# Who does the first norm's work, and where three modulation chunks stand

## The chip, the cores and the metric

The kernel runs on one core of one Trainium2 chip. The metric is the device time of one execution in microseconds, and the numbers given are medians over executions. The core has five engines that run side by side, each with its own instruction stream: TensorE (PE: matmuls, weight loads shown as PEld), VectorE (DVE), ScalarE (ACT), GpSimd (POOL) and SyncE (SP), which here only issues DMAs. They wait for each other through semaphores.

## What is computed

Two transformer-like blocks over 256 tokens of width 1024, plus a 256-token memory and a 256-token context, all in float32. What matters here, cut from the reference:

```python
h = h + _hybrid_mixer(_rmsnorm(h, mix_norm_w[l]), positions, w_in[l], ...)      # first block
h = h + _memory_cross_attn(_rmsnorm(h, xattn_norm_w[l]), mem_n, wq, wk, wv, wo)
h = h + _conv_ffn(_rmsnorm(h, ffn_norm_w[l]), ffn_up[l], ffn_conv_w[l], ffn_down[l])

def _rmsnorm(x, w):
    return (x * lax.rsqrt(jnp.mean(x * x, axis=-1, keepdims=True) + EPS)) * w

def _memory_cross_attn(h, mem_n, wq, wk, wv, wo):                                # 4 heads of 256
    q, k, v = h @ wq, mem_n @ wk, mem_n @ wv
    return softmax(q @ k.T * 256 ** -0.5) @ v @ wo

def adaln(cvec, w_mod, b_mod):                   # second block: 9 * 1024 columns for each of 2 layers
    return jax.nn.silu(cvec) @ w_mod + b_mod
```

The hybrid mixer's first branch (retention) rotates its queries and keys by angles from `positions`.

## The kernel before, in words

Activations lie feature-major: 8 tiles (`k`) of 128 features by 256 tokens. Weights come from HBM as chunks of 128x2048 floats (1 MB) through one ring of three raw slots; SP issues one DMA for each chunk, in a fixed list (`loads`, built from `plan` and `MODS_BEHIND`). To reach float32 accuracy each weight chunk `raw` is split in two: ScalarE writes the rounded `w_hi` (`split_hi`, L234), VectorE the remainder `w_lo` (`split_lo`, L242). Activations are split in the same way into `xn_hi` and `xn_lo`, and every product is three matmuls (L258 to L260): 48 for a chunk of two output tiles at 256 tokens. A raw slot is free for the next DMA once `lo_ready` has counted its chunk (L219 ff.), so VectorE's place in its own stream decides when SP may issue a load.

Each engine's stream is an order written out by hand. No planner is behind it. The prologue:

- SP: residual `xc`, eight small tables (`START`), chunks 0, 1, 2, the memory `xc[C]`, chunk 3 (waits for `lo_ready` 1), chunk 4 (waits for `lo_ready` 2), and right behind chunk 4 the nine mixer tables (`load_mixer_tables`, L529; the last is `gt<-in_pos`, the positions).
- ScalarE: eight squares (L344), `w_hi` of chunks 0 and 1, root table load and first guess (L388, L390), its square (L392), `xn_hi` for 8 tiles (L401), `w_hi` of chunk 2, squares of the memory.
- GpSimd: adds of the first norm's squares (L369; with `direct=5` two adds, and the rest is summed by TensorE), later five adds for the memory norm.
- TensorE: sum over partitions with a matrix of -1 (L373 for the added tile, L376 once for each tile that was not added), then chunk 0 tile by tile as `xn_lo` arrives, chunk 1, the memory norm's sum, chunk 2, the retention's turned products (L584, L585), and `v_tok` transposes (L591), which wait for ScalarE's copy of chunk 2 (L1403).
- VectorE: `w_lo` of chunks 0 and 1, one Newton step (L413, L415), then a scale (L431) and a low part (L438) for each k, `w_lo` of chunk 2, then the retention angles (L539 to L545), whose first step waits for all nine mixer tables.

The modulation matrix `w_mod` is read as 72 chunks (`mod`, L1644: eight small matmuls each), in six groups of 12, put between other stages by `MODS_BEHIND`: `{name: {c: (count, ahead)}}` means that `count` of them run behind chunk `c` of that job, and that their loads stand `ahead` chunks later in the list. Three stand behind the first attention (`wq` chunk 3), three within `a1_up0` (behind its chunks 2 and 5). `Attention.pe` runs eight units (4 heads, 2 token tiles each) in this order for unit u: scores of u+2, transposes of u, for even u values of head u/2-1. It has a hook `after_unit(u)`.

Of the kernel before, what the change touches and what calls it, by code (L numbers as in the profile page):

```python
# [41 lines left out]
ACT = mybir.ActivationFunctionType  # L42
# [6 lines left out]
KT = D // P  # L49
# [21 lines left out]
MODS_BEHIND = {  # L71
    "w_in_g": {3: (12, 2)},
    "wk": {3: (1, 1)},
    "wq": {3: (3, 2)},
    "wo": {3: (2, 2)},
    "ffn_down1": {7: (3, 2)},
    "a1_up0": {2: (2, 1), 5: (1, 1)},
    "a1_up1": {c: (2, 1) for c in (3, 7)},
    "a1_down1": {0: (2, 1), 3: (2, 1), 5: (1, 1), 7: (3, 2)},
    "ab_u": {1: (3, 2)},  # L80
# [9 lines left out]
def mods_behind(name, c):  # L90

    return MODS_BEHIND.get(name, {}).get(c, (0, 1))[0]
# [36 lines left out]
def build(nc, io, plan):  # L129
# [23 lines left out]
    with ExitStack() as ctx:  # L153
# [31 lines left out]
        X = slice(0, T)  # L185
# [5 lines left out]
        def col(name, k=0):  # L191
            return small[:, cols[name] + k:cols[name] + k + 1]
# [12 lines left out]
        def landed(load):  # L205

            at = place[load]
            return raw_landed[at % SLOTS], 16 * (at // SLOTS) + 16

        def raw_slot(load):  # L210
            return place[load] % SLOTS
# [14 lines left out]
        def split_hi(act, g):  # L226

            if g >= total:
                return
            slot, size = g % SLOTS, sizes[g]  # L230
            act.wait_ge(*landed(("main", g)))
            if g >= SLOTS:
                act.wait_ge(chunk_done, g + 1 - SLOTS)
            act.activation(w_hi[:, slot, 0:size], raw[:, raw_slot(("main", g)), 0:size], ACT.Copy).then_inc(hi_ready, 1)  # L234

        def split_lo(dve, g):

            if g >= total:
                return
            slot, size = g % SLOTS, sizes[g]  # L240
            dve.wait_ge(hi_ready, g + 1)
            dve.tensor_tensor(w_lo[:, slot, 0:size], raw[:, raw_slot(("main", g)), 0:size], w_hi[:, slot, 0:size].bitcast(F32),  # L242
                              ALU.subtract).then_inc(lo_ready, 1)

        def first_splits(eng, split):

            for g in range(2):
                split(eng, g)

        def bank_free(pe, s):  # L250

# [68 lines left out]
        class Norm:  # L320

            made, scaled, split, squared, added = 0, 0, 0, 0, 0
# [289 lines left out]


        _, XT, NT, QT, _, BR, GR, RT = (area(i * 1024, 8) for i in range(8))


# [91 lines left out]
        def delta_pool(pool):  # L708
            need(pool, "gdn_dve", "unit")
            pool.memset(XT, 0.0).then_inc(inverse_zero, 1)  # L710
# [202 lines left out]
        def delta_pe_u0(pe, o):  # L913
            pe.wait_ge(level_x, 15)
            pe.wait_ge(inverse_full, 4)
            for h, _, f in heads4:
                mm = pe.matmul(psum[:, 3, f], XT[:, h, :], v_tok[:, 0, f], start=True, stop=True)
            o(mm, "u0")
# [13 lines left out]
        def delta_pe_u1(pe, o):  # L932
            need(pe, "gdn_dve", "rest")
            for h, _, f in heads4:
                mm = pe.matmul(psum[:, 1, f], XT[:, 4 + h, :], REST[:, f], start=True, stop=True)
            o(mm, "u1")
# [177 lines left out]
        def gated_pool_first(pool):  # L1114
            pool.wait_ge(n_lo, memory.split_base + KT)
            pool.memset(resets, 1.0).then_inc(resets_set, 1)
            pool.wait_ge(resets_set, 1)
            pool.memset(resets.rearrange("p (b l) -> p b l", l=RUN)[:, :, 0], 0.0).then_inc(resets_set, 1)
# [512 lines left out]
        def mods_pe(pe, n):  # L1631


            for m in range(mods_run[0], mods_run[0] + n):
                group, j = m // MOD_GROUP, m % MOD_GROUP
                if j == 0:
                    if m == 0:
                        pe.wait_ge(mod_act, 1)
                    else:
                        pe.wait_ge(mod_taken, group)  # L1640
                pe.wait_ge(*landed(("mod", m)))
                for k in range(KT):
                    q = slice(32 * (k % 4), 32 * (k % 4) + 32)
                    mm = pe.matmul(psum[q, 7, 0:256], c_pad[:, k, C_AT - 2 * j:C_AT - 2 * j + 32],  # L1644
                                   raw[:, raw_slot(("mod", m)), k * 256:(k + 1) * 256],
                                   start=(j == 0 and k < 4), stop=(j == MOD_GROUP - 1 and k >= 4), tile_position=(0, 32 * (k % 4)),
                                   skip_group_check=True)
                    if k >= 4:
                        mm.then_inc(mod_used, 1)
            mods_run[0] += n  # L1650
# [534 lines left out]
        k_all = qk12[:, 8:12, :].rearrange("p (h w) t -> p h (w t)", w=2)  # L2185


        first = Norm(X, lambda k, h: col("mix_norm_w", k), direct=5)
        memory = Norm(C, lambda k, h: col("mem_norm_w", k), tiles=2, pool_low=True)
        cross = Norm(X, lambda k, h: col("xattn_norm_w", k), tiles=2)  # L2190
        ffn = Norm(X, lambda k, h: col("ffn_norm_w", k), tiles=2, early_table=True, first_tile=0)
# [12 lines left out]
        att1 = Attention(4, 2, T, lambda h, i: q1[:, 2 * h + i, :], lambda h, i: k1[:, 2 * h + i, :], lambda h, j: v1[:, j, h * T:(h + 1) * T])  # L2204
# [7 lines left out]
        @block.sync  # L2212
        def _(sp):
            sp.dma_start(xc[:, :, X], io["x"]).then_inc(residual_in, 16)
            for name in START:
                sp.dma_start(START[name][:], io[name]).then_inc(start_in, 16)
            for at in range(len(loads)):
                load(sp, at)
                if at == SLOTS - 1:
                    sp.dma_start(xc[:, :, C], io["mem"]).then_inc(mem_in, 16)  # L2220
                if loads[at] == ("main", 4):
                    load_mixer_tables(sp)

            sp.wait_ge(out_ready, 1)
            sp.dma_start(io["out"][:, 0:KT // 2, :], nrm[:, 0:KT // 2, X]).then_inc(out_in, 16)
            sp.wait_ge(out_in, 32)

        @block.tensor
        def _(pe):
# [92 lines left out]
            cross.ready(pe, KT - 1)  # L2322
            pe_feature_major(pe, jobs["wq"], xn_hi, xn_lo, X)
            pe.wait_ge(evacuated, jobs["wq"].base + jobs["wq"].n)
            att1.pe(pe)
            mods_pe(pe, mods_behind("wq", 3))
            pe.wait_ge(at_lo, att1.heads)
            pe_feature_major(pe, jobs["wo"], xn_hi, xn_lo, X, in_halves={3: pe_tile_by_tile})
            ffn.pe(pe)
# [61 lines left out]
        def _(act):  # L2391
            act.wait_ge(residual_in, 16)
            first.act_squares(act)
            act.wait_ge(start_in, 16 * len(START))
            first_splits(act, split_hi)
            first.act_rest(act)
            act.wait_ge(mem_in, 16)
            split_hi(act, 2)
            act.wait_ge(n_lo, first.split_base + KT)
# [130 lines left out]
        def _(dve):  # L2530
            dve.memset(zeros[:, :], 0.0).then_inc(set_up, 1)
            dve.memset(c_pad[:, :, :], 0.0).then_inc(set_up, 1)
            dve.wait_ge(set_up, 2)
            first_splits(dve, split_lo)
            dve.wait_ge(start_in, 16 * len(START))
            first.dve(dve)
            ret_order, delta_order, gated_order = order(dve, "ret_dve"), order(dve, "gdn_dve"), order(dve, "gat_dve")
            split_lo(dve, 2)
            retention_dve_angles(dve, ret_order)
# [172 lines left out]

        @block.gpsimd
        def _(pool):
            first.pool(pool)
            memory.pool(pool)
            memory.pool_lows(pool)
            gated_pool_first(pool)
            delta_pool(pool)
            cross.pool(pool)  # L2720
            ffn.pool(pool)
            feed0.pool(pool, lambda: n20c.pool(pool))
            n20.pool(pool)
            feed1.pool(pool)
            n21.pool(pool)
            n22.pool(pool)
            feed2.pool(pool)
            n23.pool(pool)
            feed3.pool(pool)
            n24.pool(pool)  # L2730
            n25.pool(pool)
            feed4.pool(pool)
            last.pool(pool)
# [223 lines left out]
```

## Time and profile before

| | |
|---|---|
| median of 3 runs | 2179.31 us (2178.08 to 2181.6) |
| profiled execution | 2182.45 us, its span 2180.6 us |
| PE busy | 2108.1 us, 97% of the span |
| DVE, ACT, POOL busy | 984.9, 817.2, 224.7 us |
| chain that ended last | PE 87%, DVE 7%, ACT 3%, issue 2% |
| mean granted TensorE clock | 0.991 |
| DMA | 313.97 MB, mean 144 GB/s |

The span is what the profile covers; the 1.8 us between it and the execution's own time lie around it. Busy times are sums over the whole span and say nothing on one stage. TensorE is busy nearly always, so what counts is the few places where it is not, or where its granted clock is 0.50 instead of 1.00.

### The profile page before, as it was taken

How to read it: one execution, taken by the hardware profiler on the slowest of the kernel's cores; microseconds unless marked ns; L12 is line 12 of the kernel's file. 1: busy time of each engine (PE TensorE's matmuls, PEld its weight loads, DVE VectorE, ACT ScalarE, POOL GpSimd, SP SyncE). 2: the span in 40 equal slices, each digit the busy share in tenths (PEclk: the TensorE clock that was granted, in tenths of full speed). 3: DMA queues.
4: the chain of work that ended last, by engine and by line, in shares of the span. 5: the costliest groups of instructions: out<-in, count | busy, mean ns of one | idle time of the engine just before them, and what ended most of it. 6: DMA issues, size and time to landing. Idle time of an engine off the chain costs nothing.

```text
span 2180.6 us, 31782 instructions
## 1 busy us (share of the span) xinstructions
PE 2108.1 (97%) x13882; PEld 1818.8 (83%) x13882; DVE 984.9 (45%) x1270; ACT 817.2 (37%) x1044; POOL 224.7 (10%) x185
## 2 busy tenths in 40 slices
PE   7988999999999999999999999999999999999998
PEld 6985998999978888788887888888778888869998
DVE  6677555767522322354542332243232235645444
ACT  5642454555522222243332222233212224445344
POOL 1000001413101001100101001111000110001001
PEclk9999999999999999999999999999999999999999
DMA  6425544554641243452343332243334222364543
GB/s 235 154 79 195 202 183 174 170 186 155 225 149 67 104 154 114 157 196 97 126 164 129 114 115 81 87 161 135 136 125 154 75 81 100 117 251 155 166 178 112
DMA packets 53707, 313.97 MB, mean 144 GB/s; under 512 B 5952, under 2 KB 12352, under 8 KB 23744
## 3 DMA queue, kind: packets, MB, share of 16 engines
q1 hardware_dynamic: 50848, 308.98, 39.8%
q10 hardware_dynamic: 2720, 2.95, 0.4%
q8 instruction: 109, 1.79, 0.3%
q14 instruction: 30, 0.25, 0.0%
HBM read 310.86 MB, written 1.05 MB: 143 GB/s over the span
## 4 chain that ended last, share of the span: by engine, by line
PE 87%; DVE 7%; ACT 3%; issue 2%; DMA 0%; SPq 0%; POOL 0%; DVEq 0%; ACTq 0%; POOLq 0%
PE psum L258 26%; PE psum L259 26%; PE psum L260 26%; PE psum L1644 3%; DVE w_lo L242 2%; ACT w_hi L234 2%; PE psum L1293 1%; PE psum L1283 1%; DVE work L431 0%; PE psum L1307 0%; DMA raw<-in_w_in_r 0%; DVE work L719 0%; DVE xn_lo L1809 0%; PE psum L895 0%; PE psum L1712 0%
## 5 line engine op out<-in xcount | busy, mean ns | idle before, releaser
L258 PE MATMUL psum<-xn_hi,w_hi 128*128 128x256 f32 (+1 forms) x2600 | 863.9, 332 | 22.1 <-DVE xn_lo L438 7.8
L259 PE MATMUL psum<-xn_lo,w_hi 128*128 128x256 f32 (+1 forms) x2600 | 853.1, 328 | 0.0
L260 PE MATMUL psum<-xn_hi,w_lo 128*128 128x256 f32 (+1 forms) x2600 | 852.7, 328 | 0.0
L242 DVE TENSOR_TENSOR w_lo<-raw,w_hi 128x2048 fp32r<-128x2048 f32 (+1 forms) x246 | 510.0, 2074 | 456.5 <-ACT w_hi L234 455.6
L258 PEld LDWEIGHTS psum<-xn_hi,w_hi 128*128 128x128 f32 x2600 | 496.4, 191 | 78.5 <-issue 25.5
L259 PEld LDWEIGHTS psum<-xn_lo,w_hi 128*128 128x128 f32 x2600 | 496.8, 191 | 42.6 <-issue 1.0
L260 PEld LDWEIGHTS psum<-xn_hi,w_lo 128*128 128x128 f32 x2600 | 496.5, 191 | 42.3
L234 ACT ACTIVATE w_hi<-raw 128x2048 fp32r<-128x2048 f32 (+1 forms) x246 | 421.7, 1714 | 219.6 <-PE psum L260 136.6
L258 PE MATMUL psum<-h_hi,w_hi 128*128 128x512 f32 (+1 forms) x913 | 314.9, 345 | 1.8 <-POOL h_lo L1619 1.7
L259 PE MATMUL psum<-h_lo,w_hi 128*128 128x512 f32 (+1 forms) x913 | 313.2, 343 | 0.0
L260 PE MATMUL psum<-h_hi,w_lo 128*128 128x512 f32 (+1 forms) x913 | 313.1, 343 | 0.0
L1619 POOL TENSOR_TENSOR h_lo<-work,h_hi 128x512 fp32r<-128x512 f32 (+1 forms) x110 | 154.6, 1406 | 1146.8 <-ACT h_hi L1551 1146.8
L1540 ACT ACTIVATE work<-psum 128x512 f32<-128x512 f32 (+1 forms) x88 | 47.9, 544 | 476.9 <-PE psum L260 476.8
L1589 DVE TENSOR_TENSOR work<-work,psum 128x512 f32<-128x512 f32 (+1 forms) x88 | 54.7, 621 | 373.2 <-ACT work L1540 373.1
L258 PEld LDWEIGHTS psum<-h_hi,w_hi 128*128 128x128 f32 x913 | 171.7, 188 | 27.0 <-issue 2.5
L259 PEld LDWEIGHTS psum<-h_lo,w_hi 128*128 128x128 f32 x913 | 171.8, 188 | 22.5
L260 PEld LDWEIGHTS psum<-h_hi,w_lo 128*128 128x128 f32 x913 | 171.7, 188 | 22.4
L1474 DVE SCALAR_TENSOR_TENSOR xc<-psum,mods,xc 128x256 f32<-128x256 f32 x126 | 55.7, 480 | 184.8 <-PE psum L260 184.5
L369 POOL TENSOR_TENSOR work<-work 128x256 f32<-128x256 f32 (+1 forms) x60 | 62.2, 1037 | 722.6 <-ACT work L360 673.1
L360 ACT ACTIVATE work<-xc 128x512 f32<-128x512 f32 (+2 forms) x42 | 26.1, 622 | 187.6 <-DVE xc L1474 166.3
L1551 ACT ACTIVATE h_hi<-work 128x512 fp32r<-128x512 f32 (+1 forms) x110 | 60.1, 547 | 81.4 <-DVE work L1589 81.4
L1644 PE MATMUL psum<-raw,c_pad 128*32 128x256 f32 x1152 | 73.6, 383 | 0.0
(374 smaller groups left out, 1334.0 us busy)
## 6 DMA issues: line engine op xcount, KB each, us to landing
raw<-in_mod SPq DMA_DIRECT2D x72, 1024.0 KB, 4.8
raw<-in_a_up SPq DMA_DIRECT2D x42, 1024.0 KB, 4.9
raw<-in_b_up SPq DMA_DIRECT2D x42, 1024.0 KB, 4.8
raw<-in_ffn_up SPq DMA_DIRECT2D x22, 1024.0 KB, 4.8
raw<-in_a_down SPq DMA_DIRECT2D x32, 704.0 KB, 4.1
raw<-in_b_down SPq DMA_DIRECT2D x32, 704.0 KB, 4.1
raw<-in_ffn_down SPq DMA_DIRECT2D x16, 704.0 KB, 4.2
raw<-in_wo SPq DMA_DIRECT2D x8, 1024.0 KB, 4.8
```

Of the source, the lines that this page charges most:

```text
L234: act.activation(w_hi[:, slot, 0:size], raw[:, raw_slot(("main", g)), 0:size], ACT.Copy).then_inc(hi_ready, 1)
L242: dve.tensor_tensor(w_lo[:, slot, 0:size], raw[:, raw_slot(("main", g)), 0:size], w_hi[:, slot, 0:size].bitcast(F32), ALU.subtract).then_i ...
L258: pe.matmul(out, lh, rh, start=first, stop=False, skip_group_check=group)
L259: pe.matmul(out, lh, rl, start=False, stop=False, skip_group_check=group)
L260: return pe.matmul(out, ll, rh, start=False, stop=last, skip_group_check=group)
L369: pool.tensor_tensor(nrm[:, 0, 0:self.w], nrm[:, 0, 0:self.w], nrm[:, k, 0:self.w], ALU.add).then_inc(n_added, 1)
L1474: mm = dve.scalar_tensor_tensor(x, got, gate[:, tile, h], x, ALU.mult, ALU.add)
L1540: act.activation(b[r, 0, 0:self.w], psum[r, s.bank, 0:self.w], ACT.Silu).then_inc(ff_gate, 1)
L1551: act.activation(out, b[r, 1:2, 0:self.w], ACT.Copy).then_inc(ff_hi, 1)
L1589: dve.tensor_tensor(b[r, 1, 0:self.w], b[r, 0, 0:self.w], up[up_r], ALU.mult).then_inc(evacuated, 1)
L1619: pool.tensor_tensor(lo, b[r, 1:2, 0:self.w], hi.bitcast(F32), ALU.subtract).then_inc(ff_lo, 1)
L1644: mm = pe.matmul(psum[q, 7, 0:256], c_pad[:, k, C_AT - 2 * j:C_AT - 2 * j + 32], raw[:, raw_slot(("mod", m)), k * 256:(k + 1) * 256], star ...
```

## The change

In the prologue VectorE adds the first norm's squares, six adds where GpSimd had two, so that TensorE sums two tiles in place of six. ScalarE loads its root table and makes the guess and its square ahead of both weight splits, which now stand between the high parts. VectorE does the Newton step and three scales ahead of its first weight split, and the second weight split stands behind the fifth low part. Separately, three modulation chunks move from `a1_up0` to the first attention: one behind each of units 4, 5 and 6, and three behind the attention as before.

```diff
@@ MODS_BEHIND
-    "wq": {3: (3, 2)},
+    "wq": {3: (6, 2)},
-    "a1_up0": {2: (2, 1), 5: (1, 1)},
@@ the norms
-        first = Norm(X, lambda k, h: col("mix_norm_w", k), direct=5)
+        first = Norm(X, lambda k, h: col("mix_norm_w", k), direct=1, early_table=True)
@@ tensor
-            att1.pe(pe)
-            mods_pe(pe, mods_behind("wq", 3))
+            att1.pe(pe, lambda u: mods_pe(pe, 1) if 4 <= u < 7 else None)
+            mods_pe(pe, mods_behind("wq", 3) - 3)
@@ scalar
-            first_splits(act, split_hi)
-            first.act_rest(act)
+            act.activation(col("tables", first.j), col("freq"), ACT.Abs_reciprocal_sqrt)
+            first.act_guess(act)
+            split_hi(act, 0)
+            first.act_high(act, range(0, 2))
+            split_hi(act, 1)
+            first.act_high(act, range(2, KT))
@@ vector
-            first_splits(dve, split_lo)
+            first.pool(dve)
             dve.wait_ge(start_in, 16 * len(START))
-            first.dve(dve)
+            first.dve_stats(dve)
+            for k in range(3):
+                first.dve_scale(dve, k)
+            split_lo(dve, 0)
+            for k in range(KT):
+                first.dve_low(dve, k)
+                if k + 3 < KT:
+                    first.dve_scale(dve, k + 3)
+                if k == 4:
+                    split_lo(dve, 1)
@@ gpsimd
-            first.pool(pool)
```

Line numbers after the change are six lower around the norms (L431 becomes L425, L438 becomes L432), one lower at the splits (L242 becomes L241).

VectorE's stream at the start, before (the third row holds `w_lo` of chunks 0 and 1):

```order
L2531 MEMSET zeros 128x256
L2532 MEMSET c_pad 128x432
L242 TENSOR_TENSOR w_lo<-raw,w_hi 128x2048 x2
L413 SCALAR_TENSOR_TENSOR half<-psum,half 128x256
L415 SCALAR_TENSOR_TENSOR rstd<-half,rstd 128x256
L431 SCALAR_TENSOR_TENSOR work<-xc,small,rstd 128x256 x2
L438 TENSOR_TENSOR xn_lo<-work,xn_hi 128x256
```

The same place after the change, up to the first low part, and further on from the last scale to the first step of the angles (`gt` holds the positions):

```order
L363 TENSOR_TENSOR work<-work 128x256 x6
L407 SCALAR_TENSOR_TENSOR half<-psum,half 128x256
L409 SCALAR_TENSOR_TENSOR rstd<-half,rstd 128x256
L425 SCALAR_TENSOR_TENSOR work<-xc,small,rstd 128x256 x3
L241 TENSOR_TENSOR w_lo<-raw,w_hi 128x2048
L432 TENSOR_TENSOR xn_lo<-work,xn_hi 128x256
...
L425 SCALAR_TENSOR_TENSOR work<-xc,small,rstd 128x256
L241 TENSOR_TENSOR w_lo<-raw,w_hi 128x2048
L432 TENSOR_TENSOR xn_lo<-work,xn_hi 128x256 x3
L241 TENSOR_TENSOR w_lo<-raw,w_hi 128x2048
L533 CAST work<-gt 128x256
```

The `w_lo` of chunk 1, which stood ahead of the whole norm, now stands behind the last scale; the order of everything from `w_lo` of chunk 2 on is as it was. SP's stream, after the change as before it, is the following between chunk 3 and chunk 5 (`w_in_d` x2 are chunks 3 and 4):

```order
L223 DMA raw<-in_w_in_d 128x2048 x2
L523 DMA minus_head<-in_minus_head 128x128
L523 DMA head_rows<-in_head_rows 128x168
L523 DMA in_run<-in_in_run 128x128
L523 DMA triu<-in_triu 128x128
L523 DMA tril_strict<-in_tril_strict 128x128
L523 DMA second_half<-in_second_half 128x384
L523 DMA decay<-in_decay 128x1024
L523 DMA gk_up<-in_gk_up 128x128
L523 DMA gt<-in_pos 128x256
L223 DMA raw<-in_w_in_d 128x2048
```

Nothing moved in it; the nine tables stand behind the load of chunk 4.

TensorE in the first attention from unit 4 on, before (L1283 scores, L1307 transposes, L1293 values, L1644 modulation) and after (the same four are L1277, L1301, L1287, L1638):

```order
L1307 MATMUL psum<-ident,work 128x128 x2
L1293 MATMUL psum<-work,z 128x256 x4
L1283 MATMUL psum<-z 128x256 x2
L1307 MATMUL psum<-ident,work 128x128 x4
L1293 MATMUL psum<-work,z 128x256 x4
L1307 MATMUL psum<-ident,work 128x128 x2
L1293 MATMUL psum<-work,z 128x256 x4
L1644 MATMUL psum<-raw,c_pad 32x256 x24
```

```order
L1301 MATMUL psum<-ident,work 128x128 x2
L1287 MATMUL psum<-work,z 128x256 x4
L1638 MATMUL psum<-raw,c_pad 32x256 x8
L1277 MATMUL psum<-z 128x256 x2
L1301 MATMUL psum<-ident,work 128x128 x2
L1638 MATMUL psum<-raw,c_pad 32x256 x8
L1301 MATMUL psum<-ident,work 128x128 x2
L1287 MATMUL psum<-work,z 128x256 x4
L1638 MATMUL psum<-raw,c_pad 32x256 x8
L1301 MATMUL psum<-ident,work 128x128 x2
L1287 MATMUL psum<-work,z 128x256 x4
L1638 MATMUL psum<-raw,c_pad 32x256 x24
```

The first of the three added chunks stands ahead of the scores of unit 7, the second ahead of the transposes of unit 6, the third ahead of those of unit 7.

## Rows read from the trace of the kernel before

**Rows 1.** Waits of TensorE, 20 to 135 us: total, times, longest (us)

```profile
PE psum L258 <- DVE xn_lo L438: 6.2, 1, 6.2
PE psum L837 <- DVE work L727: 2.9, 1, 2.9
...
PE psum L591 <- ACT z L1403: 0.9, 1, 0.9
```

**Rows 2.** Chain that ended last, 20 to 60 us: start, duration (us), what

```profile
29.05 0.76 DVE work L539
...
33.96 0.42 ACT work L579
...
43.11 0.59 ACT z L1403
43.74 0.66 PE psum L591 x4
...
53.03 1.62 PE psum L599 x16
```

**Rows 3.** Timeline of the prologue: start, duration (us), engine, line, what, idle before

```profile
6.38 2.56 ACT L344 ACTIVATE work<-xc 128x256 f32<-128x256 f32 x8 [4.36 <-DMA xc<-in_x]
...
9.92 4.47 PE L376 MATMUL psum<-work,minus 128*128 128x256 f32 x10
...
13.33 4.64 DVE L242 TENSOR_TENSOR w_lo<-raw,w_hi 128x2048 fp32r<-128x2048 f32 x2 [11.74 <-ACT w_hi L234]
...
17.06 0.46 ACT L390 ACTIVATE rstd<-psum,small 128x256 f32<-128x256 f32 x1
...
19.99 0.43 DVE L438 TENSOR_TENSOR xn_lo<-work,xn_hi 128x256 fp32r<-128x256 f32 x1
...
20.57 0.55 PE L258 MATMUL psum<-xn_hi,w_hi 128*128 128x256 f32 x1 [6.17 <-DVE xn_lo L438]
```

**Rows 4.** Timeline of SP's queue, 0 to 60 us

```profile
15.65 2.67 SPq L224 DMA_DIRECT2D raw<-in_w_in_d  x2
...
22.44 0.44 SPq L529 DMA_DIRECT2D gt<-in_pos  x1
```

**Rows 5.** DMA issues: count, KB each, us to landing (chunk 5; positions; a late table)

```profile
raw<-in_w_in_d SPq DMA_DIRECT2D x1, 1024.0 KB, 5.0
...
gt<-in_pos SPq DMA_DIRECT2D x1, 128.0 KB, 5.1
...
ax_cos<-in_ax_cos ACTq DMA_DIRECT2D x1, 128.0 KB, 2.0
```

**Rows 6.** Timeline of GpSimd and VectorE, 26 to 38 us

```profile
27.32 5.86 POOL L369 TENSOR_TENSOR work<-work 128x256 f32<-128x256 f32 x5 [18.53 <-ACT work L344]
...
26.76 2.29 DVE L242 TENSOR_TENSOR w_lo<-raw,w_hi 128x2048 fp32r<-128x2048 f32 x1 [1.38 <-ACT w_hi L234]
...
31.60 0.85 DVE L543 TENSOR_SCALAR work<-work 128x256 f32<-128x256 f32 x1
...
36.62 0.29 DVE L551 TENSOR_SCALAR work<-work 128x256 f32<-128x256 f32 x1
```

**Rows 7.** Stretches: us, busy (x) of PE, PEld, DVE, ACT, POOL, PEclk, DMA, GB/s

```profile
20.50:24.50 4.00, 3.93 (x18) 3.96 (x19) 4.00 (x12) 2.09 (x5) 0.00 (x0) 0.50 1.00 378
24.50:28.70 4.20, 4.20 (x37) 4.20 (x36) 2.68 (x3) 4.20 (x6) 1.38 (x1) 0.98 0.50 190
...
82.80:84.00 1.20, 1.20 (x8) 1.20 (x7) 1.20 (x1) 1.19 (x2) 0.00 (x0) 0.50 0.66 280
```

**Rows 8.** Timeline of the first attention, units 6 and 7, and the modulation behind it

```profile
330.24 0.41 DVE L1354 TENSOR_REDUCE small<-psum 128x1 f32<-128x256 f32 x1
...
331.35 0.44 PE L1307 MATMUL psum<-ident,work 128*128 128x128 f32 x2 [1.31 <-DVE work L1369]
...
336.41 2.80 PE L1644 MATMUL psum<-raw,c_pad 128*32 128x256 f32 x48
```

**Rows 9.** Timeline of TensorE in `a1_up0`, one modulation chunk behind chunk 5

```profile
641.92 1.07 PE L1644 MATMUL psum<-raw,c_pad 128*32 128x256 f32 x16
```

More of the change, by code:

```diff
@@ L243, in split_lo @@
                               ALU.subtract).then_inc(lo_ready, 1)
-        def first_splits(eng, split):
-            for g in range(2):
-                split(eng, g)
         def bank_free(pe, s):
```

## The prediction, made before the changed kernel was run

> **What bounds the kernel now.** TensorE is busy 97% of the span, so I looked first for where it stands still near the two edits, in its waits: 6.2 us ahead of the first weight matmul, 0.9 us ahead of the transposes L591, 2.9 us at L837 [rows 1]. The first of these is what the prologue edit seems to be worth. Whether it is, the chain of waits tells. Followed back from L591 at 43.74 it does not go to the early matmuls. It goes to ScalarE's copy of chunk 2 at 43.11, which stands behind the memory norm, and that behind the sines at 33.96, which wait for VectorE's angles, begun at 29.05 [rows 2]. From 43.74 TensorE works without a pause until the scores L599 at 53.03, and the chain goes through them and on to the DVE-bound wait at L837. So the prologue's end is worth what it moves L591, and that hangs on the six angle steps: when they begin and how fast they run. TensorE's own matmuls of chunks 0 to 2 have 0.9 us to spare before L591 and no more weight than that.
>
> **Prologue: when TensorE starts.** The second square is done at 7.1 (eight in 2.56 us from 6.38). A two-input 128x256 step takes VectorE 0.43, about 0.46 with its semaphore; six make 2.8, so the adds end at 9.9. TensorE did ten half-passes of such a sum in 4.47; now four are left, so the sum is there at about 12.0, and the guess, at 17.06 before, stands at 12.05 [rows 3]. The first scale follows 2.0 later as it did, three of them end at 15.3, and `w_lo` of chunk 0 takes 2.3 (two in 4.64): 17.5. Its `w_hi`, begun behind the guess's square at 12.95, is ready by 14.9. The first matmul comes 0.58 behind the start of the first low part as before: 18.05 against 20.57. So TensorE starts 2.5 us earlier. VectorE's steps of this part follow each other at 0.36 (11 starts in 4.00 us) [rows 7], so the fifth low part and the last scale are done at 21.1, and `w_lo` of chunk 1 at 23.35. TensorE is at its lower clock at first (18 matmuls in 4.00 us against 37 in 4.20) [rows 7] and waits some 0.5 us for the sixth low part. Chunks 0 to 2 and the turned products end about 2.1 us earlier, at 40.8 against 42.9.
>
> **Prologue: what is late next.** The load of chunk 4 waits for `w_lo` of chunk 1. That was done at 18.0, in the middle of the two issues that begin at 15.65 and take 2.67; it is 23.4 now, 5.4 us later, and the nine tables are queued behind that load. The positions, issued at 22.44 (4.45 behind chunk 4), are issued at 27.8 [rows 4]. They landed 5.1 after issue; a table on an empty queue took 2.0. That bounds the landing by 29.8 and 32.9 [rows 5]. I take 31.5: a 1 MB load on an empty queue took 5.0 [rows 5], so chunk 4 is there at 28.4, and the nine tables, 1.27 MB by their shapes, take 3.1 more at about 400 GB/s (378 in the stretch of rows 7, where the queue was full). VectorE, done with `w_lo` of chunk 2 at 26.7, stands idle until then. The angles begin 2.5 us later than at 29.0.
>
> **Prologue: what is faster.** GpSimd's five adds of the memory norm lay beside the angles, 27.32 to 33.2. In that time a one-input step took 0.85, and the same form 0.29 once they were over [rows 6]. After the change the memory's squares begin 24.5 in place of 26.6, so the adds run from 25.2 and are over by 31.1 even at the old pace, before the angles begin. The six steps took 4.9 (29.05 to 33.96, rows 2). Alone they take 0.33 each for three one-input steps, 0.46 each for two two-input ones, and 0.45 for the cast, which I bound by the two rows, 0.29 and 0.85: 2.35. The angles then end at 33.85, where they ended at 33.9. The late tables and the gone neighbour cancel: L591 moves by -0.1 us.
>
> The Trainium skill (GPSIMD Engine Reference, the specification table) says that GpSimd's way to SBUF is shared with VectorE, with contention for VectorE's two-port modes and for steps with two SBUF inputs. The trace agrees for the one-input steps, which it would call a two-port mode, and not for the other half: the two-input `w_lo` beside the adds took its usual 2.29 [rows 6]. By that rule alone `w_lo` of chunk 2, which now lies beside the adds too, might be slowed; it hides before the late tables, so the sum stays.
>
> **Prologue: the clock.** TensorE now has about 2.85 us without work ahead of L591 (40.8 to 43.65), before 0.9. The one wait of such a length in the same stretch, 2.9 us at L837 [rows 1], was followed by a granted clock of 0.50, that is 1.2 GHz [rows 7]. At that level a stretch of work takes twice as long; 3 to 4 us of it cost 1.5 to 2. I take 1.5. It lies on the path, since TensorE has no pause between L591 and L599. Bounds: 0 (no fall) and 2.0 (the 4 us stretch of rows 7). Prologue in sum: -0.1 + 1.5 = +1.4; from -1.8 (tables at 29.8, no fall) to about +3.5 (tables at 32.9, 2.0 for the clock).
>
> **Modulation.** In `a1_up0` TensorE does nothing but matmuls back to back. A modulation chunk there took 1.0 [rows 9] and some 0.05 around it; three take 3.0 and are saved. Behind the attention three took 2.7 (336.41 to 339.1), 0.87 each [rows 8]. Inside, the first stands ahead of the scores of unit 7. Their row maximum is what VectorE did at 330.24 ahead of normalising unit 6, for which TensorE waited 1.31 at 331.35 [rows 8]. So the first delays that chain by its whole 0.87 and hides nothing; the second then lies in the 1.31 wait and is hidden; the third delays the values of the last head, less some 0.2 of the wait there. The attention grows by 1.5. The loads: the third added chunk frees its slot at about 335.2, so the last modulation chunk lands at 340.1, while TensorE could take it at 339.6; 0.4 is waited. 1.9 less 3.0 is -1.1 us. Bounds: -3.0 (all hidden) and 0 (none, and the load late).
>
> **Sum.** +1.4 - 1.1 = +0.3 us against the profiled execution: 2182.45 + 0.3 = 2182.75. That execution lies 3.1 above the median of the runs, so I forecast 2179.31 + 0.3, rounded down to 2179.5.
>
> **Rivals.**
>
> 1. The tables only cost their latency. With an almost empty queue `gt` lands 2.0 behind its issue, at 29.8; the angles end at 32.2, L591 is 1.7 earlier and the idle time before it 1.3 us, near the 0.9 of before [rows 1], so the clock should stay up. -1.8 - 1.1: 2176.4. For: all nine are small. Against: 5.0 for one load alone on the queue, and they are behind one. [...] Chance 15%.
> 2. Slower: the angle steps keep their 4.9 us, since what slowed them was the queue's or ScalarE's traffic and not GpSimd. Tables at 31.5, angles end at 36.4, L591 is 2.5 later; TensorE is idle 5.5 us and the clock costs 2.0. +4.5 - 1.1 = +3.4: 2182.7, and 2184.1 with the tables at 32.9. It decides at any pace above 0.6 for a one-input step without GpSimd. Against it stands the 0.29 row. Chance 15%.
> 3. The gain that the wait promises: 2.5 us of earlier start arrive at L591, because the tables do not matter. -2.5 - 1.1: 2175.7. Against: VectorE waits for all nine by its code, and SP cannot issue them before 23.4. Chance 5%.
> 4. The attention does not take the three chunks (late loads or a longer chain), and the modulation edit gives nothing: +1.4: 2180.7. Chance 10%.
>
> **How the numbers follow.** The forecast has 55%. A difference under 0.2%, 4.4 us, is what a measurement of this kernel can hardly tell from none; 2175.0 to 2183.7 is that band. The forecast and rivals 3 and 4 lie inside it, rival 1 too, rival 2 reaches over its upper edge. The later clock falls may shift with the phase, by 1.5 each. So: same 0.80, faster 0.10, slower 0.10. The range is 2175.7 to 2183.5: rival 3's time below, a late rival 2 above.
>
> **What would show it.** Right: the first weight matmul near 18; chunk 4 issued near 23.4 and the positions near 27.8; VectorE idle for 4 to 5 us ahead of the cast; one-input angle steps of 0.3; L591 near 43.6 behind a longer wait, and a clock of 0.50 right after; six modulation chunks behind and in the attention that end 1.9 later, against the attention's start; `a1_up0` 3.0 shorter. Wrong: the cast right behind `w_lo` of chunk 2; steps of 0.85; L591 off by over 1.5 us; a new wait in `a1_up0` or in `wo`.

## The result, and the profile after

The changed kernel takes 2183.26 us (median of 20 executions, 2180.27 to 2186.95) against 2179.49 (20, 2176.83 to 2182.95) for the kernel before on the same chip. The ratio is 1.0015, with a 95% interval of [1.0008, 1.0021] (every ratio below is given in this way). By the ratio that is some 3.3 us more, by the medians 3.8. A later comparison gave 2183.34 against 2179.8, 1.0013 [1.0004, 1.0021]. That is within 0.2%, just inside the upper end of the forecast range (2183.5), and real: the interval excludes 1.

The two profiled executions alone don't show it: that of the changed kernel took 2181.04 us, less than that of before (2182.45). So they are compared stage by stage. Lines of the changed kernel stand 6 lower than before around the norms (L585 is what L591 was, L593 the scores L599, L831 the old L837).

The timeline of the prologue after (start, duration in us, engine, line, operation, idle before), against [rows 3], [rows 4] and [rows 6]:

```profile
6.61 2.56 ACT L338 ACTIVATE work<-xc 128x256 f32<-128x256 f32 x8 [4.58 <-DMA xc<-in_x]
7.44 3.07 DVE L363 TENSOR_TENSOR work<-work 128x256 f32<-128x256 f32 x6 [5.85 <-ACT work L338]
...
12.74 0.47 ACT L384 ACTIVATE rstd<-psum,small 128x256 f32<-128x256 f32 x1 [2.06 <-PE psum L370]
...
15.91 2.29 DVE L241 TENSOR_TENSOR w_lo<-raw,w_hi 128x2048 fp32r<-128x2048 f32 x1
...
21.77 2.28 DVE L241 TENSOR_TENSOR w_lo<-raw,w_hi 128x2048 fp32r<-128x2048 f32 x1
```

```profile
18.23 6.18 SPq L223 DMA_DIRECT2D raw<-in_w_in_d  x2
```

```profile
25.80 5.59 POOL L363 TENSOR_TENSOR work<-work 128x256 f32<-128x256 f32 x5 [25.36 <-ACT work L338]
```

The guess is there 4.3 us earlier (12.74 for 17.06), and TensorE's first weight matmul starts at 18.68 for 20.57. But `w_lo` of chunk 1 ends at 24.05, and the second of SP's two loads, chunk 4, goes out then: its issue row runs from 18.23 to 24.41. The chain that ended last (start, duration, what), against [rows 2], shows what follows:

```profile
24.08 0.33 SPq L223
...
28.26 4.26 DMA gt<-in_pos
32.54 0.30 DVE work L533
...
34.37 0.43 DVE work L539
34.83 0.43 ACT work L573
...
43.98 0.59 ACT z L1397
44.61 1.12 PE psum L585 x4
...
56.51 1.62 PE psum L593 x16
```

The table queue begins at 24.45 behind chunk 4, the positions are issued at 28.26 and land 4.3 later, and only then does VectorE begin the angles. Its six steps take 2.3 us (32.54 to 34.83) where before they took 4.9. From the end of the angles to the transposes it is 9.78 us in both kernels (33.96 to 43.74, 34.83 to 44.61). So L585 is 0.9 late. From it to the scores it is another matter: 9.29 us before (43.74 to 53.03), 11.90 now. The stretches (busy and count of PE, PEld, DVE, ACT, POOL, then granted clock, DMA share, GB/s) say why, and the waits of TensorE (total, times, longest) say what came ahead:

```profile
PE psum L585 <- ACT z L1397: 3.2, 1, 3.2
PE psum L831 <- DVE work L721: 2.8, 1, 2.8
```

```profile
44.60:49.00 4.40, 4.39 (x21) 4.39 (x22) 2.61 (x2) 1.76 (x1) 0.98 (x2) 0.50 0.02 7
49.00:53.00 4.00, 4.00 (x30) 4.00 (x30) 3.90 (x4) 0.00 (x0) 0.00 (x0) 0.81 0.80 268
```

After 3.2 us without work TensorE runs at a granted clock of 0.50 (1.2 GHz) until about 50.5, 21 matmuls in 4.4 us.

The first attention after (timeline of TensorE), against [rows 8]:

```profile
318.55 2.86 PE L1277 MATMUL psum<-z 128*128 128x256 f32 x12 [0.75 <-ACT z L1433]
...
330.84 1.07 PE L1638 MATMUL psum<-raw,c_pad 128*32 128x256 f32 x16
...
333.12 1.07 PE L1638 MATMUL psum<-raw,c_pad 128*32 128x256 f32 x16
334.13 0.44 PE L1301 MATMUL psum<-ident,work 128*128 128x128 f32 x2
...
336.23 1.07 PE L1638 MATMUL psum<-raw,c_pad 128*32 128x256 f32 x16
...
338.15 1.99 PE L1287 MATMUL psum<-work,z 128*128 128x256 f32 x8 [0.47 <-ACT work L1315]
340.07 1.93 PE L1638 MATMUL psum<-raw,c_pad 128*32 128x256 f32 x32
343.07 1.07 PE L1638 MATMUL psum<-raw,c_pad 128*32 128x256 f32 x16 [1.07 <-DMA raw<-in_mod]
344.08 0.39 PE L252 MATMUL psum<-xn_hi,w_hi 128*128 128x256 f32 x1
```

From the first scores to the first `wo` matmul it takes 25.53 us. Before it took 22.52, by these two rows of the same view:

```profile
316.61 2.86 PE L1283 MATMUL psum<-z 128*128 128x256 f32 x12 [0.75 <-ACT z L1439]
...
339.13 0.39 PE L258 MATMUL psum<-xn_hi,w_hi 128*128 128x256 f32 x1
```

To see what each stage is worth I followed one kind of instruction, VectorE's weight splits (246 in each kernel, always in the same order), and took the difference of the n-th start in two traces. Three pairs, before and after, in us: split 8, 61.59 and 65.08 (+3.5); split 34, just ahead of the attention, 312.63 and 314.58 (+2.0); split 88, behind `a1_up0`, 701.02 and 702.75 (+1.7). The modulation edit is the last step, -0.2. Rows of the third pair (VectorE, before and after):

```profile
701.02 2.20 DVE L242 TENSOR_TENSOR w_lo<-raw,w_hi 128x1408 fp32r<-128x1408 f32 x1
```

```profile
702.75 2.20 DVE L241 TENSOR_TENSOR w_lo<-raw,w_hi 128x1408 fp32r<-128x1408 f32 x1
```

The drop from +3.5 to +2.0 lies at 83 us, where before has a stretch at 0.50 [rows 7] and after has none. Past 1800 us three more such stretches differ in place and length, and the difference ends at -1.4. Those are the ways in which one execution differs from the next, as the second pair of profiles shows below.

### The profile page after: what moved, and what is told of

It is laid out like the page before. It is cut to its first block, busy times and chain, and to the rows that moved or that the text cites. A ratio compares the mean times of both kernels' runs of the same rounds, so it can differ in the third digit from the quotient of the medians.

```text
span 2179.2 us, 31773 instructions
## 1 busy us (share of the span) xinstructions
PE 2102.7 (96%) x13874; PEld 1814.2 (83%) x13874; DVE 983.9 (45%) x1276; ACT 816.5 (37%) x1044; POOL 222.5 (10%) x183
## 4 chain that ended last, share of the span: by engine, by line
PE 85%; DVE 7%; ACT 4%; issue 2%; DMA 1%; SPq 0%; DVEq 0%; ACTq 0%
PE psum L252 26%; PE psum L254 25%; PE psum L253 25%; PE psum L1638 3%; DVE w_lo L241 2%; ACT w_hi L233 2%; PE psum L1287 1%; PE psum L1277 1%; DMA raw<-in_mod 0%; DVE work L425 0%; PE psum L1301 0%; DVE work L713 0%; DVE xn_lo L1803 0%; PE psum L889 0%; DVE work L994 0%
## 5 line engine op out<-in xcount | busy, mean ns | idle before, releaser
L241 DVE TENSOR_TENSOR w_lo<-raw,w_hi 128x2048 fp32r<-128x2048 f32 (+1 forms) x246 | 509.8, 2073 | 435.9 <-ACT w_hi L233 435.1
L1638 PE MATMUL psum<-raw,c_pad 128*32 128x256 f32 x1152 | 74.0, 383 | 1.4 <-DMA raw<-in_mod 1.4
```

## The experiments

### The prologue alone, the modulation alone

Prologue alone: the kernel before with the edits of the prologue. Modulation alone:

```diff
-    "wq": {3: (3, 2)},
+    "wq": {3: (6, 2)},
-    "a1_up0": {2: (2, 1), 5: (1, 1)},
-            att1.pe(pe)
-            mods_pe(pe, mods_behind("wq", 3))
+            att1.pe(pe, lambda u: mods_pe(pe, 1) if 4 <= u < 7 else None)
+            mods_pe(pe, mods_behind("wq", 3) - 3)
```

> The changed prologue alone; the modulation chunks stand as in the kernel before. Theory (late tables, then the clock): the tables land near 32.5 us, the transposes L591 start 0.9 us later than before (near 44.6), TensorE's clock falls in the wait ahead of them, and the time is 2 to 4 us above the kernel before, as for the whole change. Rival (the modulation move is what costs): this one is at or below the kernel before, by up to 2 us, and the other half carries the loss.

> The three modulation chunks moved into the attention alone; the prologue is as before. Theory: the attention, from its first scores to the first matmul of wo, grows by 3.0 us (1.0 for each chunk inside, 0.9 saved of a wait, 1.1 waited for the last chunk's load and the rest behind), a1_up0 loses 3.0, and the time is within 1 us of the kernel before. Rival (the move is what costs): 2 us or more above it. My forecast had 1.1 us below.

The prologue alone: 2182.92 us against 2180.94, 1.0011 [1.0002, 1.0020]. Its timeline:

```profile
33.56 0.29 DVE L534 CAST work<-gt 128x256 f32<-128x256 int32 x1 [6.39 <-DMA gt<-in_pos]
```

```profile
45.63 1.12 PE L586 MATMUL psum<-ident,z 128*128 128x128 f32 x4 [4.34 <-ACT z L1398]
```

Here the positions landed 5.4 behind their issue at 28.17, so the transposes came 1.9 late, not the expected 0.9. But the clock was at 0.50 for half as long, and the scores stood near the same place as in the whole change, +3.2 against before (split 8: +3.2).

The modulation alone: 2178.6 us against the same 2180.94, 0.9996 [0.9988, 1.0005]. The attention grew by 3.1, split 88 against split 34 is -0.3, and the same load was waited for:

```profile
340.42 1.07 PE L1643 MATMUL psum<-raw,c_pad 128*32 128x256 f32 x16 [1.15 <-DMA raw<-in_mod]
```

So the whole loss is the prologue's, and the modulation edit is worth nothing that can be measured.

### The tables behind chunk 3 instead of chunk 4

The whole change with one more line, and the prologue alone with the same line:

```diff
-                if loads[at] == ("main", 4):
+                if loads[at] == ("main", 3):
                     load_mixer_tables(sp)
```

> The whole change, with the nine mixer tables issued behind chunk 3 in place of chunk 4. Theory: the positions are issued near 23.1 us and are there before VectorE has done w_lo of chunk 2 (27.3); the angles run beside GpSimd's five adds at 0.85 for a one-input step and end near 32.2 in place of 34.8; L591 comes near 42.0, with under 1.5 us of idle time ahead of it and the clock still up; the time is 1 to 3 us below the kernel before and 4 to 6 below the changed one. Rival (the tables are not what L591 waits for): no more than 1 us below the changed kernel. Second rival (the angle steps are slow or fast by the DMA traffic beside them): they take 0.3 here too and end near 29.6.

> The changed prologue with the tables behind chunk 3, and the modulation chunks as before. Theory: the same as with the whole change and early tables within 1 us, since the modulation move gives nothing: 1 to 3 us below the kernel before. If the modulation move costs, this one is the best of all by 1 us or more; if it gains its 1.1, it is 1 us above the one with the whole change.

The whole change with the line takes 2178.88 us, 0.9991 [0.9982, 0.9999], and the prologue alone with it 2178.16, 0.9989 [0.9981, 0.9998], both against 2180.94. One line turns the loss into a small gain; so it was the tables' place in the queue. The two are alike, so here too the modulation edit gives nothing. The timeline of the first:

```profile
24.96 2.29 DVE L241 TENSOR_TENSOR w_lo<-raw,w_hi 128x2048 fp32r<-128x2048 f32 x1
27.16 0.29 DVE L533 CAST work<-gt 128x256 f32<-128x256 int32 x1
27.49 0.71 DVE L534 TENSOR_SCALAR work<-work,small 128x256 f32<-128x256 f32 x1
28.24 0.85 DVE L536 TENSOR_SCALAR work<-work 128x256 f32<-128x256 f32 x1
...
30.00 0.97 DVE L538 SCALAR_TENSOR_TENSOR work<-work 128x256 f32<-128x256 f32 x1
```

```profile
41.67 0.66 PE L585 MATMUL psum<-ident,z 128*128 128x128 f32 x4 [0.30 <-ACT z L1397]
```

```profile
41.70:45.00 3.30, 3.30 (x28) 3.30 (x29) 1.54 (x1) 1.72 (x1) 0.95 (x2) 1.00 0.02 7
```

The angles start behind `w_lo` of chunk 2 without waiting, beside GpSimd's adds (25.79 to 31.57), and all but the cast are slow again: 4.7 us for the six. Even so L585 comes 2.1 earlier than before, TensorE waits 0.3, and its clock stays up.

### How long the angle steps take without GpSimd's adds

The kernel before, with one addition on GpSimd for the memory norm instead of five (TensorE sums the rest):

```diff
-        memory = Norm(C, lambda k, h: col("mem_norm_w", k), tiles=2, pool_low=True)
+        memory = Norm(C, lambda k, h: col("mem_norm_w", k), tiles=2, direct=6, pool_low=True)
```

> The kernel before, with GpSimd adding one tile for the memory norm in place of five; TensorE sums seven in place of three. Theory (GpSimd's adds are what doubled the angle steps): L540, L542 and L543 take near 0.3 us in place of 0.85, the six steps 2.3 to 3 in place of 4.9, though the tables are as early as before. Rival (the DMA traffic or ScalarE beside them): they stay at 0.85.

One profile, 2180.29 us. VectorE's and GpSimd's rows:

```profile
28.79 0.83 DVE L539 CAST work<-gt 128x256 f32<-128x256 int32 x1
29.66 0.35 DVE L540 TENSOR_SCALAR work<-work,small 128x256 f32<-128x256 f32 x1
30.05 0.29 DVE L542 TENSOR_SCALAR work<-work 128x256 f32<-128x256 f32 x1
...
30.71 0.42 DVE L544 SCALAR_TENSOR_TENSOR work<-work 128x256 f32<-128x256 f32 x1
```

```profile
27.14 2.33 POOL L369 TENSOR_TENSOR work<-work 128x256 f32<-128x256 f32 x1 [18.30 <-ACT work L344]
```

The cast, which overlaps the end of the one addition (29.47), is slow; everything behind it is at the fast pace, and the six steps take 2.8 us. On VectorE nothing was changed, so GpSimd's adds are what slows them. Two-input steps too: 0.42 here, 0.97 beside the adds. In return GpSimd's addition took 2.33 while `w_lo` ran beside it. An addition without `w_lo` beside it takes 0.74; this is the third of the five in the kernel before:

```profile
30.68 0.74 POOL L369 TENSOR_TENSOR work<-work 128x256 f32<-128x256 f32 x1
```

There the two engines take turns: the slow one-input steps end at 30.69, 31.57 and 32.45, and the next additions begin at 30.68, 31.56 and 32.45. So a small step beside the adds takes about as long as one add.

This kernel shows only the pace of the steps. Its transposes L591 came 1.1 us later than before, with no wait ahead of them, since TensorE had the longer sum (2.75 us for 1.03) and was itself the last to be ready.

### The wait before L585 filled with work

The whole change, and three needless matmuls (into a free bank) between the turned products and the transposes:

```diff
             retention_pe_turned(pe, ret_order)
+            for _ in range(3):
+                pe.matmul(bank(5), rot[:, :], decay[:, 0:2, :], start=True, stop=True)
             retention_pe_values(pe, ret_order)
```

> The whole change, with three needless matmuls (128x512, into an unused bank) between the turned products and the v_tok transposes, in the time in which TensorE otherwise waits; their results are used by nothing. Theory (the tables cost 0.9 us, the clock the larger part): the matmuls take 0.9 each and end before the copy of chunk 2, the transposes start near 44.6 us as in the changed kernel, but the clock is still up, so the scores L593 come 9.3 us behind them (53.9) in place of 11.9 (56.5); the time is 1.5 to 3 us below the changed kernel. Rival (the clock is not what costs; the loss is the later start alone): no more than 0.5 us below the changed kernel, and the scores near 56.5.

It took 2182.42 us against 2181.93, 1.0005 [0.9996, 1.0014].

```profile
41.50 2.74 PE L2235 MATMUL psum<-decay,rot 128*128 128x512 f32 x6
44.90 0.66 PE L585 MATMUL psum<-ident,z 128*128 128x128 f32 x4 [0.66 <-ACT z L1397]
```

```profile
45.00:49.00 4.00, 4.00 (x35) 4.00 (x36) 2.32 (x2) 1.64 (x1) 0.87 (x2) 1.00 0.00 0
```

The transposes came no earlier (44.90 against 44.61), but the clock stayed at 1.00, the scores stood 9.27 behind them instead of 11.90, and split 8 is at +1.1 instead of +3.5. Idle time ahead of L585 costs more than itself: here the clock's part was 2.6, the larger of the two terms. The median moved the right way, but its interval holds both 1 and the changed kernel's ratio; the term's size rests on the traces.

### Two chunks inside the attention, with the early tables

```diff
-    "wq": {3: (3, 2)},
+    "wq": {3: (5, 2)},
-    "a1_up0": {2: (2, 1), 5: (1, 1)},
+    "a1_up0": {2: (1, 1)},
-            att1.pe(pe)
-            mods_pe(pe, mods_behind("wq", 3))
+            att1.pe(pe, lambda u: mods_pe(pe, 1) if u in (3, 5) else None)
+            mods_pe(pe, mods_behind("wq", 3) - 2)
```

> Changed prologue, tables behind chunk 3, and another place for the modulation: one chunk behind each of units 3 and 5 of the attention, three behind it, one left in a1_up0. Theory (a chunk is hidden only where TensorE waits for VectorE, and a late load costs): the one of unit 5 is hidden in the 1.3 us wait, the one of unit 3 is not, the loads are in time; the attention to wo grows by 1.1 us where a1_up0 loses 2.0, and the time is 0.5 to 1.5 below the kernel with early tables and the modulation as before, which the times can hardly show. Rival (any chunk inside costs its full 1.0 us): no gain.

> The same kernel as e6 once more. Its first time was 6 to 8 us below the kernel before, where its moved work explains 4.7 (as the chunks' weight splits stood at 1790 us). Theory (the rest was where the clock's falls lay late in the program, which differs between executions): the median falls back toward 4 to 6 us below the kernel before, and the profile again shows 4.7 +- 0.5 at 1790 us once the prologue's clock stretches are taken off. Rival (the other place of the modulation also takes clock falls away for good): again 6.5 us or more below.

It took 2173.59 us against 2181.93, 0.9970 [0.9958, 0.9983], and in the second comparison, of the same kernel, 2175.88 against 2179.8, 0.9982 [0.9973, 0.9990]. TensorE's timeline in the second:

```profile
324.28 1.07 PE L1639 MATMUL psum<-raw,c_pad 128*32 128x256 f32 x16
...
329.37 1.07 PE L1639 MATMUL psum<-raw,c_pad 128*32 128x256 f32 x16
330.75 0.44 PE L1302 MATMUL psum<-ident,work 128*128 128x128 f32 x2 [0.31 <-DVE work L1364]
...
335.80 2.80 PE L1639 MATMUL psum<-raw,c_pad 128*32 128x256 f32 x48
```

The chunk behind unit 5 stands where TensorE waited 1.31 us; the three behind the attention run in one piece, with no load waited for. The attention, from its first scores to `wo`, grew by only 0.5 us (22.52 to 23.06) where 1.1 was expected: the chunk behind unit 3 was partly hidden too, since the 0.45 us that TensorE waited ahead of unit 4's transposes in the kernel before (at 326.79) are gone. From split 34 to split 88 the two profiles give -1.6 each, and split 8 is at -1.9 and -2.2. Together that is 3.5 to 3.8 us; the second interval, 2.2 to 5.9 us of gain, holds it, and the first, 3.7 to 9.2, touches it. The expectation for the second run was missed: at 1790 us its weight splits are 2.8 ahead of the kernel before and not 4.7, and the median is 3.9 below it and not 4 to 6. This version beats both kernels. That it beats the two with early tables is shown by the traces' -1.6 alone, since the intervals of the times overlap with theirs. Which of its three differences from the whole change (two chunks, the other units, one load fewer) makes the modulation's gain was not tried apart.

### Both kernels profiled once more

> The kernel before once more, to see what differs between two executions of one program. Theory: the prologue and the waits fall at the same times within 0.5 us, but the stretches at the lower clock differ in place and number, and with them the span by 1 to 3 us. Rival: the same stretches as in the first profile.

> The changed kernel once more. Theory: tables near 32.5 us, L585 near 44.6 to 45.6, a stretch at the lower clock of 3.4 to 6.8 us that begins within the wait; 3 to 4 us above the kernel before in the median. Rival (the fall of the clock there was chance): the clock stays up in this profile, and the scores follow the transposes after 9.3 us.

The kernel before took 2183.99 us in its one execution. Its input landed 0.3 later and its first weight chunk 0.8, and its first stage ended later with them (split 8: +0.75 against the first profile, where at most 0.5 was expected; L591 at 44.50). The changed kernel took 2183.34 us in 12 executions (the ratio is above). Its timeline and the stretch:

```profile
33.47 0.29 DVE L533 CAST work<-gt 128x256 f32<-128x256 int32 x1 [6.31 <-DMA gt<-in_pos]
```

```profile
45.54 1.11 PE L585 MATMUL psum<-ident,z 128*128 128x128 f32 x4 [4.27 <-ACT z L1397]
```

```profile
44.60:49.00 4.40, 3.46 (x16) 3.46 (x17) 1.68 (x1) 2.69 (x3) 1.90 (x3) 0.61 0.20 84
49.00:53.00 4.00, 4.00 (x36) 4.00 (x35) 3.93 (x4) 0.00 (x0) 0.00 (x0) 1.00 0.58 184
```

The same two terms again, divided otherwise: the transposes are 1.8 late, the clock is back at 49, split 8 is at +3.3. Here the wait of 2.84 us at L831 was followed by 0.50, as before and unlike the first profile of the changed kernel: right behind it the difference is still +3.3 (split 13), where the first profile had +2.0. So the drop there was that execution's luck and no part of the change. In the twelve profiles of all kernels this wait was followed by the lower clock nine times; without it were the first of the changed kernel, one with early tables and one with two chunks inside.

## Why the prediction was right, and which terms were off

The forecast was no change within 0.2%, +0.3 us; it is +0.15% [+0.08, +0.21], about +3.3. In the prologue the mechanism was the one predicted, but it cost more than forecast; the modulation's gain did not come. By the traces the terms add up to about what was measured:

| term | predicted | first profile | second | prologue alone |
|---|---|---|---|---|
| transposes L591 move | -0.1 | +0.9 | +1.8 | +1.9 |
| clock behind them | +1.5 | +2.6 | +1.5 | +1.4 |
| modulation | -1.1 | -0.2 | -0.1 | |
| sum | +0.3 | +3.3 | +3.2 | +3.2 |

(The moves are against 43.74, the first profile of the kernel before; the clock's term is the time from the transposes to the scores less the 9.29 of before. The three profiles with the old prologue and all its adds have the transposes at 43.4, 43.7 and 44.5, so the first row is uncertain by some 0.8. The sum is clear of that: split 8 differs from the first profile by -0.3 to +0.8 in those three and by +3.2 to +3.5 with the new prologue.)

- **TensorE's earlier start.** Right that it is worth nothing. It was 1.9 us instead of 2.5: the input landed 0.2 later, six adds took 3.07 and not 2.8. With the first add 0.1 later behind its square, some 0.65 came through to `w_lo` of chunk 1, done at 24.05 for 23.4.
- **What is late next.** The mechanism was right: chunk 4 waits, and nine tables behind it. The size was off. I took the positions at 31.5; they came at 32.5, 33.5 and 33.5 in the three profiles of this prologue with unfilled wait (32.8 with it filled). Of the 1.0 to 2.0, 0.3 to 0.5 is the later issue. The rest is the landing, 4.3 to 5.4 us behind the issue, where I had allowed 3.7 by summing sizes at the queue's rate. The row of before, 5.1 [rows 5], was the better estimate, and I had chosen under it. The 2.0 of the late table was no row for this case: it went out on ScalarE's queue (ACTq), alone.
- **What is faster.** Right: six steps in 2.29 for 2.35. The rival that gave the slowing to something else fell with the one-addition kernel. That rule of the Trainium skill on the shared way to SBUF (GPSIMD Engine Reference, the specification table) named steps with two SBUF inputs too. My "not for the other half", from `w_lo` alone, was a misreading: the two-input L538 and L539 take 0.97 and 0.84 beside the adds and 0.42 without, and where `w_lo` keeps its 2.29 it is the add beside it that waits, 2.33 for 0.74.
- **The clock.** Right in kind, with a bound too low: I capped it at 2.0 by the 4 us stretch of [rows 7]. In the first profile the work behind the wait ran at the lower level from 44.6 to about 50.5. In the three profiles the two terms trade: where the tables are later, this term is smaller, and the sum to the scores is +3.2 to +3.5 each time, near the +3.5 that the prediction had as the prologue's upper bound. Why the clock comes back after another length of time was not settled.
- **Modulation.** This step failed: -1.1 was forecast, and -0.1 to -0.3 is what the traces show. The two chunks ahead of unit 6's transposes cost 0.84 (14.74 us from the first scores to them before, 15.58 now): as predicted, the 1.31 wait hides one. The third cost 0.89 and not 0.67 (from unit 6's transposes to the last values it is 4.02 us, and 3.13 before, 331.35 to 334.48): a chunk alone between other work takes 1.0, as [rows 9] had it, and I had used the 0.87 of a row of three. The last load cost 1.1 and not 0.4: its slot comes free with that third chunk at 337.2, and it lands 5.8 later, at 343.0, where I had allowed 4.9. The attention grew by 3.0 for 1.9, and `a1_up0` gave 3.2 back for 3.0. So rival 4, an edit without gain, is what held for this part.
- **Rivals.** Tables at their mere latency (29.8) and a gain of 2.5 from the early start did not occur. Rival 2's price, +3.4, was met by other means than its own: the steps ran at 0.29 to 0.35 without the adds.

Of the chances, the 0.80 for within 0.2% held. The forecast's value lies 3.8 below the measured median, since the terms together came out on the costly side of what I took: the transposes and the modulation each time, the clock in the first profile. That the median is inside the range at all is in part luck: it lies 0.2 below the upper end, which was set for rival 2, the slow steps, and that did not occur. (That end is also below the rival's own 2184.1, and the terms named for the prologue's upper bound, 1.3 and 2.0, sum to 3.3 and not 3.5.)

## What to carry to other kernels

When a step is moved ahead of another on one engine, look for the semaphore counts of the one that is pushed back: here a weight split freed a load slot, and what stood behind that load in SP's queue, not the load, was the loss; one line put it right. Do not take a landing time below what the same transfer took in the trace unless the queue ahead of it gets shorter. The waits of 3.2 to 4.3 us ahead of these transposes carried a surcharge of 1.4 to 2.6 us at the lower clock, so a small lateness there is to be priced at more than itself. And fill the waits of an engine with as many pieces as they hold, not one more. Before reading a small difference from two single profiles, profile each kernel twice: here the same stage of the same kernel moved by 0.8 us, and whole spans of one kernel differed by 1.6 to 4.4.

## What was not expected of the hardware

- The same wait in the same code is not always followed by the lower clock: 2.84 us at L831 was, in the second profile of the changed kernel (0.50 from 87.0 to 89.4), and was not in the first (1.00 from 86.0 on). It was in nine profiles of twelve.
- The lower clock lasted longer after the shorter wait: after 3.2 us until about 50.5 us, after 4.3 us until 49.
- At the start of the changed kernel TensorE works at the pace of the lower level, 20 matmuls in 4.3 us, in a stretch whose granted clock reads 1.00. So the mean granted clocks of the two kernels (0.991 and 0.994) are not to be compared.

```profile
18.70:23.00 4.30, 4.30 (x20) 4.30 (x21) 4.30 (x10) 2.79 (x6) 0.00 (x0) 1.00 0.67 244
```

- The contention of VectorE and GpSimd works both ways: a 128x256 addition on GpSimd took 2.33 us beside a 128x2048 `w_lo`, which itself kept its 2.29, while VectorE's small steps took two to three times as long beside the same adds. The cast is the exception: right behind `w_lo` it took 0.29 in three profiles with early tables, though the first add had not ended, and 0.83 in others.
- The same 128 KB table, issued at 28.1 to 28.3 behind the same transfers, landed 4.3 us later in one execution and 5.3 and 5.4 in two others. The table issued just ahead of it landed at 31.7 to 31.8 in all three, so it is the last one alone that varied. A 1 MB load is issued 0.5 behind it each time; whether that load is what delays it was not tried.
